# Moving every third split of transposed probabilities from VectorE to GpSimd in two attention stages

## What is computed

```python
# mla_attention: 8 heads, causal, q and k of 96, v of 64
sc = jnp.einsum('bqhd,bkhd->bhqk', qb, k).astype(jnp.float32) * scale
sc = jnp.where(causal[None, None], sc, -jnp.inf)
p = jax.nn.softmax(sc, axis=-1).astype(v.dtype)
return jnp.einsum('bhqk,bkhd->bqhd', p, v)
```

## Time and profile before

| | |
|---|---|
| runs shown | 3820.32, 3820.52, 3822.85 us; median 3820.52 us |
| profiled execution | 3819.39 us, span from first to last instruction 3817.6 us |
| busy over the span | PE 84%, PEld 71%, DVE 55%, ACT 47%, POOL 22% |
| mean granted TensorE clock | 0.924 of full speed |
| `mla` attention, about 724 to 1200 us | 476 us |
| `dsa` attention, about 1955 to 2420 us | 465 us |

### The profile page before, as it was taken

One profiled execution on the slowest core, in us unless ns is written; L12 is line 12 of the kernel. 1 busy time (PEld: TensorE's weight loads), 2 busy tenths in 40 slices (PEclk: granted clock), 3 DMA queues, 4 the chain that ended last, 5 costly groups with the idle time before them and its releaser, 6 DMA issues. The chain is left out here.

```text
span 3817.6 us, 51207 instructions
## 1 busy us (share of the span) xinstructions
PE 3225.2 (84%) x17416; PEld 2713.7 (71%) x17416; DVE 2086.8 (55%) x4976; ACT 1805.7 (47%) x3441; POOL 852.3 (22%) x1096
## 2 busy tenths in 40 slices
PE   3898554699995889999939999687988999969998
PEld 3796443588884677777736777566876888858997
DVE  2200898588885465556449988633215666643112
ACT  2210554476674556565537777300215666644221
POOL 2200676011112322111111100111212444421110
PEclk9999676799998999999969999898998999979999
DMA  6611477633334522222262110554535222225432
GB/s 163 229 58 61 154 232 208 155 83 67 88 65 110 169 76 69 71 83 63 74 119 47 38 29 18 178 198 146 171 118 160 67 67 67 56 69 169 127 122 67
DMA packets 375907, 411.26 MB, mean 108 GB/s; under 512 B 72896, under 2 KB 290800, under 8 KB 371936
## 3 DMA queue, kind: packets, MB, share of 16 engines
q1 hardware_dynamic: 351296, 347.30, 32.2%
q0 software_dynamic: 13408, 48.57, 4.0%
q10 hardware_dynamic: 10944, 12.13, 0.9%
HBM read 236.61 MB, written 171.31 MB: 107 GB/s over the span
## 5 line engine op out<-in xcount | busy, mean ns | idle before, releaser
L80 PE MATMUL i_p_g<-i_hT_lo,i_wh 128*128 128x512 f32 x768 | 310.9, 405 | 10.1 <-issue 7.8
L82 PE MATMUL i_p_g<-i_hT_hi,i_wh 128*128 128x512 f32 x768 | 306.5, 399 | 0.0
L81 PE MATMUL i_p_g<-i_hT_hi,i_wl 128*128 128x512 f32 x768 | 306.3, 399 | 0.0
L1569 DVE SCALAR_TENSOR_TENSOR i_score<-i_relu,i_w,i_score 128x1024 f32<-128x1024 f32 (+7 forms) x154 | 156.0, 1023 | 196.3 <-ACT i_relu L1443 194.0
L1454 ACT ACTIVATE i_above<-i_score,i_less 128x384 bf16<-128x384 f32 (+13 forms) x140 | 182.9, 1307 | 84.1 <-POOL i_less L1520 63.3
L1089 DVE TENSOR_TENSOR mla_tl<-mla_p_t,mla_th 128x512 fp32r<-128x512 f32 (+1 forms) x320 | 185.9, 605 | 45.3 <-ACT mla_th L1132 42.5
L1059 DVE CUSTOM_DVE_ANT_0 dsa_probs<-dsa_p_s,dsa_mask 128x512 f32<-128x512 f32 (+3 forms) x320 | 184.4, 604 | 42.3 <-PE dsa_p_s L1698 41.0
L1443 ACT ACTIVATE i_relu<-i_p_s 128x1024 f32<-128x1024 f32 (+7 forms) x176 | 141.7, 810 | 137.1 <-DVE i_score L1566 87.4
L1132 ACT ACTIVATE mla_th<-mla_p_t 128x512 fp32r<-128x512 f32 (+1 forms) x320 | 163.8, 529 | 88.7 <-PE mla_p_t L1029 86.3
L1089 DVE TENSOR_TENSOR dsa_tl<-dsa_p_t,dsa_th 128x512 fp32r<-128x512 f32 x272 | 179.8, 685 | 39.9 <-ACT dsa_th L1132 30.3
L1697 PE MATMUL dsa_p_s<-dsa_k_hi,dsa_q 128*128 128x512 f32 (+3 forms) x320 | 132.3, 415 | 71.6 <-DMA dsa_k_lo<-scratch_kbT 46.1
(11 more groups left out here) (358 smaller groups left out, 9845.0 us busy)
## 6 DMA issues: line engine op xcount, KB each, us to landing
scratch_gates<-i_ob SPq DMA_DIRECT2D x96, 256.0 KB, 2.1
m_m<-scratch_gates SPq DMA_DIRECT2D x64, 256.0 KB, 3.5
f_hs<-scratch_h2T SPq DMA_DIRECT2D x16, 1024.0 KB, 9.6
scratch_qkT<-b_th SPq DMA_DIRECT2D x64, 192.0 KB, 3.2
scratch_qkT<-b_tl SPq DMA_DIRECT2D x64, 192.0 KB, 3.5
i_ws<-in_w_in SPq DMA_DIRECT2D x24, 512.0 KB, 4.3
scratch_tm<-p_ob ACTq DMA_DIRECT2D x64, 137.0 KB, 1.8
b_tmb<-scratch_tm SPq DMA_DIRECT2D x16, 548.0 KB, 4.2
```

Source lines behind the costliest of these rows:

```text
L80: pe.matmul(out, l[0], r[1], start=start, stop=False)
L81: pe.matmul(out, l[1], r[0], start=False, stop=False)
L82: return pe.matmul(out, l[0], r[0], start=False, stop=stop)
L1569: nc.vector.scalar_tensor_tensor(out=acc, in0=r, scalar=w[:, t, h:h + 1], in1=acc, op0=ALU.mult, op1=ALU.add).then_inc(summed, 1)
```

## The change

Blocks with b % 3 == 2 (`by_pool`) take another way. ACT copies the `p_t` bank to a new SBUF tile `whole` (two slots) with no rounding and no wait for a free `th` slot, but a wait for `pool_lo` of the block two uses of `whole` before. GpSimd then makes both halves: `tensor_copy` from `whole` to `th`, and the subtraction `whole - th` to `tl`. DVE skips these blocks. PE waits on `pool_hi` and `pool_lo` for them instead of `hi_done` and `lo_done`, and their `p_t` bank is free once ACT has copied it (`copied`). GpSimd now walks the list of steps too: block splits and the O parts stand in one queue in the order of the list. The branches for `packed` false, which neither attention uses, are dropped.

```diff
         shift = sb("shift", [P, R, 4])
         th = sb("th", [P, S, GT], F32R)
         tl = sb("tl", [P, S, GT], F32R)
+        whole = sb("whole", [P, 2, GT])
...
+        copied, pool_hi, pool_lo = (sem(f"{tag}_{n}") for n in ("copied", "pool_hi", "pool_lo"))
+        by_pool = lambda b: b % 3 == 2
+        n_pool = lambda b: b // 3
+        n_own = lambda b: b - n_pool(b)
+
+        def wait_hi(eng, b):
+
+            if by_pool(b):
+                eng.wait_ge(pool_hi, n_pool(b) + 1)
+            else:
+                eng.wait_ge(hi_done, n_own(b) + 1)
+
+        def wait_lo(eng, b):
+
+            if by_pool(b):
+                eng.wait_ge(pool_lo, n_pool(b) + 1)
+            else:
+                eng.wait_ge(lo_done, n_own(b) + 1)
+
+        def wait_read(eng, b):
+
+            if by_pool(b):
+                eng.wait_ge(copied, n_pool(b) + 1)
+            else:
+                eng.wait_ge(lo_done, n_own(b) + 1)
...
-                pe.wait_ge(hi_done, b + 1)
+                wait_hi(pe, b)
                 out = p_o[:, n % 2, s0 * P:GT]
                 v, last = layer.values(n, j), place == len(units[n]["blocks"]) - 1
                 hi, lo = th[:, b % S, s0 * P:GT], tl[:, b % S, s0 * P:GT]
-                if layer.packed:
-                    nc.tensor.matmul(out, v, hi, start=place == 0, stop=False)
-                    pe.wait_ge(lo_done, b + 1)
-                    nc.tensor.matmul(out, v, lo, start=False, stop=last).then_inc(multiplied, 1)
...
+                nc.tensor.matmul(out, v, hi, start=place == 0, stop=False)
+                wait_lo(pe, b)
+                nc.tensor.matmul(out, v, lo, start=False, stop=last).then_inc(multiplied, 1)
...
                 else:
-                    pe.wait_ge(lo_done, r - m + 1)
+                    wait_read(pe, r - m)
...
                 elif step[0] == "B":
                     _, n, place, j, s0 = step
                     b = n_b[n] + place
-                    if b >= S:
-                        dve.wait_ge(multiplied, b - S + 1)
-                    dve.wait_ge(hi_done, b + 1)
-                    nc.vector.tensor_tensor(tl[:, b % S, s0 * P:GT], p_t[:, ring(n, place), s0 * P:GT],
-                                            th[:, b % S, s0 * P:GT].bitcast(F32),
-                                            ALU.subtract).then_inc(lo_done, 1)
+                    if not by_pool(b):
+                        if b >= S:
+                            dve.wait_ge(multiplied, b - S + 1)
+                        dve.wait_ge(hi_done, n_own(b) + 1)
+                        nc.vector.tensor_tensor(tl[:, b % S, s0 * P:GT], p_t[:, ring(n, place), s0 * P:GT],
+                                                th[:, b % S, s0 * P:GT].bitcast(F32),
+                                                ALU.subtract).then_inc(lo_done, 1)
...
                     act.wait_ge(turned, b + 1)
+                    if by_pool(b):
+                        if n_pool(b) >= 2:
+                            act.wait_ge(pool_lo, n_pool(b) - 1)
+                        nc.scalar.activation(whole[:, n_pool(b) % 2, s0 * P:GT], p_t[:, ring(n, place), s0 * P:GT],
+                                             ACT.Copy).then_inc(copied, 1)
+                        continue
                     if b >= S:
                         act.wait_ge(multiplied, b - S + 1)
                     nc.scalar.activation(th[:, b % S, s0 * P:GT], p_t[:, ring(n, place), s0 * P:GT],
...
             layer.pool_start(pool)
-            for n in range(len(units)):
-                layer.pool_unit(pool, n)
-                if layer.packed:
+            n_made = 0
+            for step in steps:
+                if step[0] == "B":
+                    _, n, place, j, s0 = step
+                    b = n_b[n] + place
+                    if by_pool(b):
+                        n_made += 1
+                        if b >= S:
+                            pool.wait_ge(multiplied, b - S + 1)
+                        pool.wait_ge(copied, n_pool(b) + 1)
+                        part = slice(s0 * P, GT)
+                        src = whole[:, n_pool(b) % 2, part]
+                        nc.gpsimd.tensor_copy(th[:, b % S, part], src).then_inc(pool_hi, 1)
+                        pool.wait_ge(pool_hi, n_pool(b) + 1)
+                        nc.gpsimd.tensor_tensor(tl[:, b % S, part], src, th[:, b % S, part].bitcast(F32),
+                                                ALU.subtract).then_inc(pool_lo, 1)
+                elif step[0] == "O":
+                    n = step[1]
+                    if n_made:
+                        pool.wait_ge(pool_lo, n_made)
                     pool.wait_ge(weighed, n + 1)
                     if n >= 1:
                         pool.wait_ge(out_done, n)
```

More of the change, by code:

```diff
@@ L950, in stage_attention @@
                                         "weighed", "out_done"))
+        copied, pool_hi, pool_lo = (sem(f"{tag}_{n}") for n in ("copied", "pool_hi", "pool_lo"))
[17 more added lines that the diff above has]
+                eng.wait_ge(lo_done, n_own(b) + 1)
         stored, lowered = sem(f"{tag}_stored", 2), sem(f"{tag}_lowered")
         n_s = [sum(-(-k // GT) for u in units[:n] for k in u["keys"]) for n in range(len(units) + 1)]
-        output_read = weighed if layer.packed else out_done
+        output_read = weighed
         layer.setup(nc, sem, ident, c, dict(exped=exped, inverted=inverted, multiplied=multiplied, moved=moved,
@@ L1101, in _ @@
                     dve.wait_ge(spread_done, n + 1)
[L1102 to L1107, removed]
                     if n >= 2:
```

## The result

The changed kernel takes 3863.66 us (median of 4 runs, 3855.51 to 3865.67), the kernel before 3820.42 us. The ratio is 1.0109 with a 95% interval of 1.0091 to 1.0126: slower by 1.1%, some 42 us (the two medians lie 43.2 us apart), outside the forecast's range of 3792 to 3850 us. Its profiled execution took 3865.67 us, 46.3 more than that of before. Nearly all of it lies in the two attentions. From the first move of scores (L1059, now L1078) to the end of the last `halves` (L1110, now L1124), `mla` took 712.6 to 1200.5 us before and takes 710.7 to 1228.8 now, 30 us more; `dsa` took 1953.3 to 2421.2 and takes 1984.9 to 2466.3, 13.5 us more.

What follows compares the result with a forecast made beforehand. PE was taken to bound `mla` with DVE not far behind, and both to be near in `dsa`. 3819.4 - 16.7 + 21.7, less 3.5 for catching up and with 1.13 us to the median, gave 3822 us, range 3792 to 3850.

Steps and rivals of the forecast that it cites:

- The price of GpSimd's work: Per moved block on GpSimd: a cast at the copy's 0.61 us and a subtraction of 1.28 us.
- the rival that GpSimd's path decides: PE waits for moved blocks' halves, above all after output steps; slower, 3848 us with the cast at 1.0 us; chance 0.29.
- No blocking: GpSimd and DVE would not block each other; the rival that they do, 3866 us, had chance 0.04.
- The relief: Time regained where PE waits for DVE: 8.6 us of bank waits plus 8.1 of score waits, 16.7 us.
- The bank waits: PE waiting for `p_t` banks held by DVE subtractions: 5.3 us regained in `mla` and 3.3 in `dsa`.
- the score waits: PE waiting for score banks at the start of a lead: 7.9 us regained in `dsa`, 0.2 in `mla`.
- I placed all 196 moved blocks against PE's old times in this way, outputs included: Count of late GpSimd splits: 22 blocks of `mla` late by 15.4 us, 16 of `dsa` by 6.3; 21.7 us.
- The place: Where splits come late: 18.3 of the 21.7 us within 4 us of an output step.
- The balance of the stages: Profile after: `mla` some 5 to 10 us longer, `dsa` some 5 to 10 us shorter.
- The sum: Whole kernel: 16.7 us gained, 21.7 lost to lateness, 3.5 taken back for engines catching up; 3822 us, no change; chance 0.40.

Runs made afterwards that it cites:

- no wait: The change, but GpSimd's output step copies and adds the unit before, so the work stays without the wait for the weighed result: 3843.67 us, ratio 1.0058.
- no work: The change, but GpSimd's output step keeps its wait and copies and adds 4 columns instead of 512: 3821.34 us, ratio 1.0018.
- no output step: The change, but GpSimd has no output step, neither wait nor work; VectorE copies 4 columns in its place: 3825.82 us, ratio 1.0026.
- the relief alone: Kernel before, every third block's subtraction left out, PE multiplying its upper half twice, nothing on GpSimd: 3806.92 us, ratio 0.9971.
- the path without the relief: The change, but VectorE still does a same-size subtraction per moved block into an unused tile, and the bank waits for it: 3875.59 us, ratio 1.0155.

## Why the prediction was wrong

- **The price of GpSimd's work** was right: 0.61 and 1.29 us. The cast was not dear. But the rival that GpSimd's path decides, which I let begin at a cast of about 0.75 us, came true at 0.61.
- **No blocking** of VectorE by GpSimd: right. `shift` took 153 to 156 ns with GpSimd at work 46% of the stage, and the large moves of scores took 606 ns in the mean of either stage, against 605 and 604 before.
- **The relief** was mis-sized: 16.7 us counted, 10 measured, and nearly all of the difference lies in `dsa` (5.6 us for 11.2; `mla` 4.7 for 5.5). The bank waits fell to about half, as forecast. The term at fault is the score waits: 7.9 us were to come back in `dsa`, and the waits of PE's weight loads there fell by 4.3.
- **The failed step** is "I placed all 196 moved blocks against PE's old times in this way, outputs included". I let GpSimd serve splits and outputs as each became ready, a choice that the prediction does not state. Its queue runs in the order of the program. A split that is ready must stand behind an output step whose `halves` are not, as block 95 does. Done again on the same old times in the order of the program, the count is 27.9 us late in `mla` and 15.6 in `dsa`, 43.5 instead of 21.7. With 10 us of relief that is 33 us slower, where 42 was measured. The 21.8 us of difference are what the order of the queue adds in the count, and taking the wait away gave back 19 us measured, 14 of standing time.
- **The place** was right in the main: 36 of 49 us stand at the 60 blocks next behind an output step, where the forecast had 18.3 of 21.7 within 4 us of one. The two runs that keep colliding blocks on VectorE or keep others there show it. The balance of the stages was wrong: `mla` was to be 5 to 10 us longer and `dsa` 5 to 10 shorter, and they are 30 and 13.5 us longer.
- **The sum** took back 3.5 us for engines that catch up. It should have gone the other way. With the work in GpSimd's queue but not the wait, the kernel is 22 us over before; with the relief of 10 that is 32 us of lateness, where the count gave 16.3. By the standing times, the count in program order is too low in each of the four runs: 43.5 for 49 us, 16.3 for 35 (no wait), 10.7 for 20 (no work), 5.4 for 17 (no output step).
- **PE's old times**, which the count took as given, are a part of the reason: with the relief, PE comes sooner. Before, the last transpose in front of the multiplication of block 80 waited for its bank; in the run of the relief alone it does not:

```profile
846.28 0.33 PE L1029 MATMUL mla_p_t<-ident,mla_probs 128*128 128x128 f32 x1 [0.63 <-DVE mla_tl L1089]
...
844.32 0.33 PE L1035 MATMUL mla_p_t<-ident,mla_probs 128*128 128x128 f32 x1
```

  It starts 1.42 us after ScalarE begins to read block 80 in the kernel before, 0.63 us after it with the relief alone, and 1.36 in the run of the path without the relief. At the 136 blocks that are not next behind an output the standing time is 8.3 us without the relief and 12.5 with it. So this is worth some 4 us; where the rest comes from stays open.
- The rule of the Trainium skill that elementwise work belongs on VectorE ("GPSIMD Engine Reference", engine selection) was borne out for this change: a subtraction takes 1286 ns on GpSimd and 689 on VectorE (`dsa`). The price as such did not decide: with the same price for each block, 136 moved blocks and a lag of 4 beat the kernel before.

## What to carry to other kernels

When work moves to an engine that has little to do, its load says nothing: walk its queue in program order, with every wait that stands in it, and ask for each new item which older wait it now stands behind. Before, the waits of such an engine cost nothing; with new work behind them they do. And the consumer's old times are no fixed mark: relief elsewhere lets it come sooner. If the items still collide, move only those that don't, or lengthen the distance to the consumer; here the two together turned 1.1% slower into 0.27% faster.

## What the runs showed of the hardware

GpSimd casts float32 to float32r at the price of its plain copy, 610 ns against 608 for 512 elements a row, and its subtraction takes 1286 ns with the result in float32r, where a two-input operation of the same size with a float32 result takes 1292. With GpSimd at work nearly half of both stages, VectorE's operations kept their length to within 4 ns (scores 604 to 606 ns in `dsa`, subtractions there 685 to 689, `halves` 679 to 680).
